# Down projection of a transformer layer as seven block products over two chunks, added to the residual out of PSUM

## What is computed

```python
def hybrid_layer(x, ...):
    ...
    x = x + mixed @ w_out
    h = rms_norm_2(x, mlp_norm_w)
    return x + jnp.square(jax.nn.relu(h @ w_up)) @ w_down
...
for layer in range(DEPTH_2):          # DEPTH_2 = 2
    x = hybrid_layer(x, ...)
return rms_norm_2(x, final_norm_w)
```

## Time and profile before

| | us |
|---|---|
| median of 3 runs | 2745.24 (2744.96 to 2747.38) |
| the profiled execution, its own time | 2742.98 |
| its span, first to last instruction | 2740.9 |
| TensorE busy in the span | 2535.8 (93%) |
| VectorE busy | 1757.3 (64%) |
| ScalarE busy | 1214.6 (44%) |
| stretch of the first layer's feed-forward part | 1676.85 to 2026.91 |
| stretch of the second layer's | 2377.20 to 2727.23 |

### The profile page before, as it was taken

The page is one execution under the profiler, slowest core; times in us unless marked ns, Lnnn a source line. Parts: engine busy times, 40 slices in busy tenths (PEclk is TensorE's granted clock), DMA queues, the critical chain, the costliest instruction groups (busy, mean ns, idle before and its releaser), DMA issues.

```text
span 2740.9 us, 32380 instructions
## 1 busy us (share of the span) xinstructions
PE 2535.8 (93%) x11843; PEld 1995.5 (73%) x11843; DVE 1757.3 (64%) x2579; ACT 1214.6 (44%) x1747; POOL 154.6 (6%) x186
## 2 busy tenths in 40 slices
PE   5899999999987999999699899999999989999998
PEld 2776877777775878787576567888887656788886
DVE  5466566786856989998648864444443886444445
ACT  5432355555333777776442463222243336423222
POOL 0111000000000111111000000000000100000000
PEclk8999999999998999999899899999999999999999
DMA  6457535454433999998334432232233443222331
GB/s 224 162 194 252 150 98 151 119 147 142 162 130 123 364 373 366 359 349 309 133 100 123 121 91 93 92 102 97 92 98 100 137 118 94 75 96 92 96 100 72
DMA packets 229560, 431.54 MB, mean 157 GB/s; under 512 B 63380, under 2 KB 86435, under 8 KB 229442
## 3 DMA queue, kind: packets, MB, share of 16 engines
q1 hardware_dynamic: 211978, 386.83, 42.7%
q0 software_dynamic: 17232, 43.02, 4.6%
q10 hardware_dynamic: 232, 0.14, 0.0%
HBM read 399.00 MB, written 46.68 MB: 163 GB/s over the span
## 4 chain that ended last, share of the span: by engine, by line
PE 63%; DVE 18%; DMA 8%; ACT 5%; issue 4%; SPq 1%; POOL 0%; DVEq 0%; ACTq 0%; POOLq 0%
PE BKP L825 29%; PE BKP L1039 5%; PE BKP L847 4%; PE BKP L845 4%; PE BKP L846 4%; DVE WL L3026 3%; DMA W<-in_w_expert_gu_dram 2%; DVE G L3140 2%; PE BKP L1169 2%; DVE TOP L3138 2%; PE BKP L1083 2%; ACT WH L1979 2%; DVE hL L3026 1%; DMA G<-in_w_expert_gu_dram 1%; PE TPP L1070 1%
## 5 line engine op out<-in xcount | busy, mean ns | idle before, releaser
L2239 DVE TENSOR_TENSOR WL<-W,WH 128x2048 fp32r<-128x2048 f32 x126 | 288.7, 2292 | 351.8 <-ACT WH L1534 349.5
L1534 ACT ACTIVATE WH<-W 128x2048 fp32r<-128x2048 f32 x126 | 241.1, 1914 | 565.2 <-PE BKP L825 284.5
L825 PE MATMUL BKP<-hH,WH 128*128 128x512 f32 x896 | 354.5, 396 | 12.0 <-ACT Z L1593 2.7
L825 PE MATMUL BKP<-hL,WH 128*128 128x512 f32 x896 | 349.4, 390 | 0.0
L825 PE MATMUL BKP<-hH,WL 128*128 128x512 f32 x896 | 348.8, 389 | 0.0
L825 PEld LDWEIGHTS BKP<-hH,WH 128*128 128x128 f32 x896 | 168.2, 188 | 59.4 <-issue 15.0
L847 PE MATMUL BKP<-WH,aL 128*128 128x512 f32 x512 | 199.2, 389 | 0.0
L845 PE MATMUL BKP<-WH,aH 128*128 128x512 f32 x512 | 199.2, 389 | 0.0
L846 PE MATMUL BKP<-WL,aH 128*128 128x512 f32 x512 | 199.2, 389 | 0.0
L825 PEld LDWEIGHTS BKP<-hL,WH 128*128 128x128 f32 x896 | 168.2, 188 | 36.0
L825 PEld LDWEIGHTS BKP<-hH,WL 128*128 128x128 f32 x896 | 168.4, 188 | 33.6
(11 more groups left out here) (573 smaller groups left out, 5534.7 us busy)
## 6 DMA issues: line engine op xcount, KB each, us to landing
W<-in_w_expert_gu_dram SPq DMA_DIRECT2D x46, 1024.0 KB, 7.5
G<-in_w_expert_gu_dram SPq DMA_DIRECT2D x46, 1024.0 KB, 7.6
W<-in_w_in_dram SPq DMA_DIRECT2D x42, 1024.0 KB, 5.2
W<-in_w_up_dram SPq DMA_DIRECT2D x32, 1024.0 KB, 5.1
W<-in_w_down_dram SPq DMA_DIRECT2D x32, 1024.0 KB, 5.1
W<-in_w_expert_down_dram SPq DMA_DIRECT2D x24, 1024.0 KB, 6.7
G<-in_w_expert_down_dram SPq DMA_DIRECT2D x22, 1024.0 KB, 6.8
X<-in_w_mod_dram SPq DMA_DIRECT2D x16, 1024.0 KB, 7.7
```

The lines of the kernel that those rows point to most:

```text
L825: mm = pe.matmul(BK[j][:, 0:cols], lt, rh, start=start and a == 0, stop=stop and a == len(q) - 1, skip_group_check=True)
L1534: act.activation(WH[s][:], W[s][:] if raw is None else raw, ACT.Copy).then_inc(sems["w_hi"], 1)
L2239: v.tensor_tensor(WL[s][:], W[s][:] if raw is None else raw, WH[s][:].bitcast(F32), ALU.subtract).then_inc(sems["w_lo"], 1)
```

## The change

Two chunks are taken together. Their down projection is a product of a 512 x 1024 matrix of hidden values and a 1024 x 1024 matrix of weights. Hidden values are cut into four blocks (chunk by half of the tokens, `HQ[chunk][half]`, 256 tokens each), weights into four (chunk by half of the output columns), and the output into four quarters of `X` (half of the tokens by half of the columns, `X11`, `X12`, `X21`, `X22`). Seven products of sums and differences of such blocks take the place of the eight direct ones. Four differences of weight blocks (`weights_made`) and four sums or differences of hidden rows (`rows_made`) are made by VectorE.

A product `q` has its own weight pair (`WH3`, `WL3`: now three places in a ring, the third on `Z` and `AT`) and its own operand pair (`OPH`, `OPL`: three places). It adds into one of three pairs of PSUM banks (`FOLD`): A is `SC`, B is `TP`, C is `BK[2]` and `BK[3]`. A chain of products goes on adding in the same bank, and after each product VectorE adds the sum as it then stands to a quarter of `X` (`to_x`). A product's two halves wait for their bank's `sc_free` or `tp_free`, which `to_x` raises.

The hidden values are now finished before they are rounded: VectorE takes max(PSUM, 0) times the token's norm factor into `HR` (`evacuated`; `RTOK` holds the factors along the columns, spread by four small matmuls and a copy), and ScalarE squares in place (`squared`). `SQUARE` becomes the root of what it was (`roots` in place of a reciprocal). Raw weight blocks go round four places (`raw_units`); differences are written over raw blocks that are no longer needed, one into `TBUF`. The loops over chunks become code written out for four pairs per layer on every engine. Between the layers the transposes of two column blocks stand ahead of the last product, two behind it (`folded_blk`). In the last layer the root and scaling of tiles 0 and 1 stand between the adds of products 5 and 6. Some semaphores are shared under new names (`op_hi`, `op_lo`, `sig_sq`, `rows_made`), and some small tensors are put side by side to get the space.

The diff, cut to its core and moved to the left (in order: names; bank pairs and raw places; SyncE; TensorE; ScalarE; VectorE):

```diff
+by4 = lambda ap: ap.rearrange("p (k n) -> p k n", k=UK)
+WH3, WL3 = [WH[0][:], WH[1][:], by4(ZR)], [WL[0][:], WL[1][:], by4(ATR)]
+HR, HQ = [ST[0], ST[1]], [[ST[c][:, :, t * 256:(t + 1) * 256] for t in range(2)] for c in range(2)]
+SA, SB3, TBUF = by4(flat(F[:])), by4(QSB[:]), by4(BIG[:, 0:UK * UN])
+OPH = [by4(flat(aH[:])[:, 0:1024]), by4(flat(aH[:])[:, 1024:2048]), by4(BIGR[:, 2048:3072])]
+OPL = [by4(flat(aL[:])[:, 0:1024]), by4(flat(aL[:])[:, 1024:2048]), by4(BIGR[:, 3072:4096])]
+RTOK = flat(VSB[:])[:, 0:S]
+GFN = flat(W[0][:])[:, 0:D]
+TBL = [TP[:, 0:512], TP[:, 512:1024], BK[2], BK[3], TP[:, 0:512], TP[:, 512:1024], SC[:, 0:512], SC[:, 512:1024]]
...
+PAIRS = ["sc_free", "tp_free"]
+NPAIR, UPAIR = FF // UN // 2, 11
+FOLD = [("A", True), ("B", True), ("A", False), ("B", False), ("A", False), ("C", True), ("A", False)]
+FOLD_BANKS = {"A": [(SC[:, 0:UN], "sc_free"), (SC[:, UN:], "sc_free")],
+              "B": [(TP[:, 0:UN], "tp_free"), (TP[:, UN:], "tp_free")],
+              "C": [(BK[2], BANKS[2]), (BK[3], BANKS[3])]}
+def raw_units(g, s):
+    ring = [(W[1 - s][:], f"w_landed{1 - s}"), (G[:, 0:4, :], "w_landed2"), (G[:, 4:8, :], "w_landed3")]
+    return (W[s][:], f"w_landed{s}"), ring[g % 3], ring[(g + 1) % 3], ring[(g + 2) % 3]
...
+def get(raw, m, src):
+    sp.wait_ge(sems["w_lo"], first + m + 2)
+    load(raw[0], src.rearrange("(k p) n -> p k n", p=P), raw[1])
+for g in range(NPAIR):
+    m = UPAIR * g
+    a, b, c, d = raw_units(g, s)
+    up = lambda ch, k: pick(t["w_up_2"], l)[k * UN:(k + 1) * UN, (2 * g + ch) * UN:(2 * g + ch + 1) * UN]
+    dn = lambda ch, hf: pick(t["w_down_2"], l)[(2 * g + ch) * UN:(2 * g + ch + 1) * UN, hf * UN:(hf + 1) * UN]
+    get(a, m - 5 if g else -2, up(0, 0))
+    get(b, m - 4 if g else -1, up(0, 1))
+    get(c, m - 2 if g else 0, up(1, 0))
+    get(d, m - 1 if g else 0, up(1, 1))
+    get(a, m, dn(0, 1))
+    get(b, m + 1, dn(0, 0))
+    get(c, m + 2, dn(1, 0))
+    get(d, m + 3, dn(1, 1))
...
+def folded(q, o, s):
+    pe.wait_ge(sems["w_lo"], T.next("w_lo"))
+    pe.wait_ge(sems["op_lo"], T.next("op_lo", 2 if q == 1 else 1))
+    banks, opens = FOLD[q]
+    for tt, (bank, free) in enumerate(FOLD_BANKS[banks]):
+        pe.wait_ge(sems[free], T.next(free))
+        cols = slice(tt * P, (tt + 1) * P)
+        for k in range(UK):
+            pe.matmul(bank, OPH[o][:, k, cols], WH3[s][:, k, :], start=opens and k == 0, stop=False,
+                      skip_group_check=True)
+            pe.matmul(bank, OPH[o][:, k, cols], WL3[s][:, k, :], start=False, stop=False, skip_group_check=True)
+            mm = pe.matmul(bank, OPL[o][:, k, cols], WH3[s][:, k, :], start=False, stop=k == UK - 1,
+                           skip_group_check=True)
+        mm.then_inc(sems["gemm_done"], 2)
...
+def folded_blk(form, n):
+    def rest(j):
+        if j == 0:
+            pe.wait_ge(sems["x4"], 3 * NT)
+            for k in range(4, NK):
+                turned_x(k, TBL[k])
+    for k in (2, 3):
+        pe.wait_ge(sems[BANKS[k]], T.at(BANKS[k]))
+        turned_x(k, TBL[k])
     unit(h, 0, form, n, True, False, ready="norm_lo", each=rest)
...
+def factors_spread(j):
+    if j == 0:
+        pe.wait_ge(sems["norm_rd"], 2 + 2 * l + 2)
+        for i in range(NT):
+            mm = pe.matmul(SC[:, i * P:(i + 1) * P], SQUARE[:, i:i + 1].to_broadcast([P, P]), IDN[:],
+                           start=True, stop=True, skip_group_check=True)
+        mm.then_inc(sems["row_pe"], 1)
+        T.skip("row_in")
+for g in range(NPAIR):
+    m = UPAIR * g
+    if g == 0:
+        normed_blk(at=(at(0), at(1)), each=factors_spread)
+    else:
+        unit(h, 0, "F", UN, True, False, at=at(m))
+        unit(h, 4, "F", UN, False, True, at=at(m + 1))
+    unit(h, 0, "F", UN, True, False, at=at(m + 2))
+    unit(h, 4, "F", UN, False, True, at=at(m + 3))
+    for q in range(7):
+        if g == NPAIR - 1 and q == 6 and l == 0:
+            pe.wait_ge(sems["norm_xn"], T.next("norm_xn", NT))
+            for k in range(2):
+                turned_x(k, TBL[k])
+        folded(q, (7 * g + q) % 3, at(m + 4 + q))
...
+def rounded(m, src):
+    act.wait_ge(sems["gemm_done"], g0 + (1 if m == 2 else 4 * (m - 2)))
+    act.activation(WH3[ring[m % 3]], src, ACT.Copy).then_inc(sems["w_hi"], 1)
+def squared(c, j):
+    act.wait_ge(sems[BANKS[j]], T.next(BANKS[j]))
+    act.activation(HR[c][:, j, :], HR[c][:, j, :], ACT.Square).then_inc(sems["sig_sq"], 1)
+def operand(g, q, src, made, ks=slice(0, UK)):
+    n = 7 * g + q
+    if n >= 3:
+        act.wait_ge(sems["gemm_done"], g0 + 4 * (UPAIR * g + (q + 2 if q >= 3 else q - 2)))
+    if made:
+        act.wait_ge(sems["rows_made"], T.next("rows_made", made))
+    act.activation(OPH[n % 3][:, ks, :], src[:, ks, :], ACT.Copy).then_inc(sems["op_hi"], 1)
...
+rounded(m + 3, d[0])
+if g == 0:
+    landed(b, c)
+    T.skip("norm_rd")
+    act.wait_ge(sems["row_pe"], T.next("row_pe"))
+    act.activation(RTOK, SC[:, 0:S], ACT.Copy).then_inc(sems["row_in"], 1)
...
+landed(d)
+act.wait_ge(sems["tw_made"], T.next("tw_made", 2))
+rounded(m + 5, a[0])
+for j in range(3):
+    squared(1, j)
+operand(g, 1, SA, 2, slice(0, 2))
+squared(1, 3)
+operand(g, 1, SA, 1, slice(2, 4))
+act.wait_ge(sems["tw_made"], T.next("tw_made"))
+rounded(m + 6, a[0])
+operand(g, 2, HQ[0][0], 1)
+rounded(m + 7, c[0])
+operand(g, 3, SA, 1)
+rounded(m + 8, TBUF)
+operand(g, 4, SB3, 0)
+rounded(m + 9, d[0])
+act.wait_ge(sems["sig_sq"], T.next("sig_sq", 4))
+operand(g, 5, HQ[1][0], 0)
+act.wait_ge(sems["tw_made"], T.next("tw_made"))
+rounded(m + 10, b[0])
+operand(g, 6, HQ[1][1], 0)
...
-link(v.reciprocal(SQUARE, SM[:, 3, 0:4]))
+roots(SQUARE, m4, half4, work4)
+v.sem_inc(sems["norm_rd"], 1)
...
+def remainder(m, src):
+    v.wait_ge(sems["w_hi"], T.next("w_hi"))
+    r = ring[m % 3]
+    v.tensor_tensor(WL3[r], src, WH3[r].bitcast(F32), ALU.subtract).then_inc(sems["w_lo"], 1)
+    T.skip("w_lo")
+def evacuated(m, c, j):
+    v.wait_ge(sems["gemm_done"], g0 + 4 * m + j + 1)
+    v.scalar_tensor_tensor(HR[c][:, j, :], BK[j], 0.0, RTOK, ALU.max, ALU.mult).then_inc(sems[BANKS[j]], 1)
+    T.skip(BANKS[j])
+def operand(n, src, ks=slice(0, UK)):
+    v.wait_ge(sems["op_hi"], T.next("op_hi"))
+    v.tensor_tensor(OPL[n % 3][:, ks, :], src[:, ks, :], OPH[n % 3][:, ks, :].bitcast(F32),
+                    ALU.subtract).then_inc(sems["op_lo"], 1)
+def rows_made(dst, a, b, op, ks=slice(0, UK)):
+    v.tensor_tensor(dst[:, ks, :], a[:, ks, :], b[:, ks, :], op).then_inc(sems["rows_made"], 1)
+def weights_made(dst, a, b):
+    v.tensor_tensor(dst, a, b, ALU.subtract).then_inc(sems["tw_made"], 1)
+    T.skip("tw_made")
+x_rows = lambda first, hf: [X[:, i, hf * UN:(hf + 1) * UN] for i in (first, first + 1)]
+X11, X12, X21, X22 = x_rows(0, 1), x_rows(0, 0), x_rows(2, 1), x_rows(2, 0)
+def to_x(g, q, dst, since, last=False):
+    for tt, (bank, free) in enumerate(FOLD_BANKS[FOLD[q][0]]):
+        v.wait_ge(sems["gemm_done"], g0 + 4 * (UPAIR * g + 4 + q) + 2 * (tt + 1))
+        if tt == 0:
+            v.wait_ge(sems[since], T.at(since, 0))
+        v.tensor_tensor(dst[tt], dst[tt], bank, ALU.add).then_inc(sems[free], 1)
+        if last:
+            v.wait_ge(sems[free], T.at(free))
+            v.sem_inc(sems["x4"], 1)
+        T.skip(free)
+a, b, c, d = raw_units(0, s)
+remainder(1, b[0])
+for g in range(NPAIR):
+    last = g == NPAIR - 1
...
+if g:
+    to_x(g - 1, 6, X21, BANKS[3])
+remainder(m + 2, c[0])
+remainder(m + 3, d[0])
+if g == 0:
+    v.wait_ge(sems["row_in"], T.next("row_in"))
+else:
+    weights_made(TBUF, c[0], b[0])
+for j in range(4):
+    evacuated(m + 1, 0, j)
+remainder(m + 4, a[0])
+operand(n, HQ[0][0])
+if g == 0:
+    weights_made(TBUF, c[0], b[0])
+weights_made(a[0], b[0], a[0])
+v.wait_ge(sems["sig_sq"], T.next("sig_sq", 4))
+rows_made(SB3, HQ[0][0], HQ[0][1], ALU.subtract)
+remainder(m + 5, a[0])
+weights_made(a[0], c[0], a[0])
+evacuated(m + 3, 1, 0)
+v.wait_ge(sems["tw_made"], T.at("tw_made", 0))
+weights_made(b[0], d[0], a[0])
+evacuated(m + 3, 1, 1)
+evacuated(m + 3, 1, 2)
+v.wait_ge(sems["sig_sq"], T.next("sig_sq", 2))
+rows_made(SA, HQ[0][1], HQ[1][1], ALU.add, slice(0, 2))
+evacuated(m + 3, 1, 3)
+operand(n + 1, SA, slice(0, 2))
+v.wait_ge(sems["sig_sq"], T.next("sig_sq", 2))
+rows_made(SA, HQ[0][1], HQ[1][1], ALU.add, slice(2, 4))
+operand(n + 1, SA, slice(2, 4))
+rows_made(HQ[0][0], SA, HQ[0][0], ALU.subtract)
+remainder(m + 6, a[0])
+operand(n + 2, HQ[0][0])
+to_x(g, 0, X11, BANKS[3])
+remainder(m + 7, c[0])
+rows_made(SA, HQ[1][0], HQ[0][0], ALU.subtract)
+operand(n + 3, SA)
+to_x(g, 1, X22, "sc_free")
+remainder(m + 8, TBUF)
+operand(n + 4, SB3)
+to_x(g, 2, X12, "tp_free")
+remainder(m + 9, d[0])
+operand(n + 5, HQ[1][0])
+to_x(g, 3, X12, "sc_free", last)
+remainder(m + 10, b[0])
+operand(n + 6, HQ[1][1])
+to_x(g, 4, X22, "tp_free", last)
+if not last:
+    a, b, c, d = raw_units(g + 1, s)
+    remainder(m + 11, a[0])
+    to_x(g, 5, X11, "sc_free")
+    remainder(m + 12, b[0])
+elif l == 0:
```

(47 more changed lines are left out.)

244 lines of the change are left out of this document (134 added, 110 removed).

## The result

The changed kernel takes 2701.78 us (2699.00 to 2704.97), the kernel before 2745.1 beside it: a ratio of 0.9844, 95% interval 0.9830 to 0.9858. Two later sets of executions of the same kernel gave 0.985 (0.9828 to 0.9873) and 0.9864 (0.9846 to 0.9883). The forecast was 2705.4 in 2700 to 2720, that is 39.8 us less.

What follows compares the result with a forecast made beforehand. TensorE was taken to bound both MLPs throughout. Terms -43.5 (matmuls) +3 (waits) +1.8 (row factors) +0 (boundary) -1.1 (end) gave -39.8 us, a profiled execution of 2703.2 and a median of 2705.4, range 2700 to 2720.

Steps and rivals of the forecast that it cites:

- TensorE alone bounds both parts, and 192 matmuls are 43.5 us: Both MLPs: TensorE is busy throughout; 24 fewer matmuls per pair, 5.44 us each, over 8 pairs save 43.5 us.
- Waits, 3 us, at q=3 alone: TensorE waits before q=3 on VectorE's add: 0.2 us per pair, 0.5 in each layer's first; sum 2.2, taken as 3.
- The walk: Step-by-step timing of VectorE and ScalarE through one later pair; it found q=3 the tightest place, 0.2 us late.
- Rival A: VectorE's overlap between operations is lost at semaphore waits: waits 10.6 us instead of 3, about 2713 us; chance 0.20.
- Rivals B: ScalarE's handoffs to VectorE are not covered: 1.23 us each, 15 per pair, 120 in all, 2822 us; chance 0.06.
- C: Uncovered handoffs in part, or late loads or fetches, eat 4 us or more per pair: 2716 to 2739; chance 0.10.
- D: Such losses eat 5.4 us per pair and nothing changes: within 5.5 us of 2745; chance 0.04.
- Row factors, 1.8: Four small matmuls and a copy per layer spread the row factors, holding TensorE 0.92 us: +1.8 us for two layers.
- Between the layers 0: Boundary between the layers: 5.85 us before, 5.9 walked after, so zero change, plus or minus 1.5 us.
- at the end -1.1: After TensorE stops, the last scaling ends 9.6 us later instead of 10.7: -1.1 us, between -2.5 and +1.
- Strided operand reads at the plain price: VectorE reads operands as rows of 256 out of 512 columns; priced like plain reads, nothing added.
- of the same form: The products' 168 matmuls per pair match the old 192 in form (128x128 stationary, 512 columns), each priced at 0.2267 us.

Runs made afterwards that it cites:

- experiment 2: Changed kernel with each pair's first product computed twice, putting back 24 matmuls per pair: MLPs +21.78 and +21.67 us, ratio 1.0007 to the kernel before.
- experiment 5: Changed kernel with MODP, CF and KS0 moved so ATR begins at 128 modulo 8192: each MLP 1.65 us less; in a later run 2700.16 us against 2703.17.
- experiment 3: Changed kernel with one more VectorE instruction per pair, a 128x1024 sum of 1.21 us ahead of the q=1 adds to X: 2711.77 us against 2701.97.
- experiment 4: Changed kernel with MODP moved ahead of F, so ATR begins at a multiple of 64 bytes: second layer's MLP 331.4 to 331.1 us, ratio 0.9836 to the kernel before.

## Why the prediction was right, step by step

**TensorE alone bounds both parts, and 192 matmuls are 43.5 us.** Right, to 0.1: experiment 2 puts them back for 43.45.

**Waits, 3 us, at q=3 alone.** The place was right, the size was not: by the starts the changed kernel waits 0.07 or less around q=3 in each pair, 0.25 in both layers. This is the term that was mis-sized, and two things lie under it. The walk took 0.75 us for an evacuation, from the nearest row with a scalar per partition; groups of the kernel after, with the columns of the earlier trace rows:

```profile
L3432 DVE SCALAR_TENSOR_TENSOR ST<-BKP,VSB 128x512 f32<-128x512 f32 x64 | 42.4, 684 | 26.3 <-PE BKP L875 19.5 <-ACT VSB L2303 6.8
L3456 DVE TENSOR_TENSOR X<-X,SCP 128x512 f32<-128x512 f32 x64 | 41.7, 680 | 4.3 <-PE SCP L911 3.5 <-DVE X L3456 0.2
```

At 0.684 the walk, which has four of them ahead of the adds of q=1, has these adds 0.2 to 0.3 earlier. In a later pair that starts at 1759.00, VectorE in fact does this (timeline):

```profile
1811.33 1.28 DVE L3456 TENSOR_TENSOR X<-X,SCP 128x512 f32<-128x512 f32 x2
1812.53 2.28 DVE L3426 TENSOR_TENSOR WL<-G,WH 128x2048 fp32r<-128x2048 f32 x1
1814.73 1.22 DVE L3442 TENSOR_TENSOR F<-ST 128x1024 f32<-128x1024 f32 x1
1817.13 1.23 DVE L3438 TENSOR_TENSOR aL<-F,aH 128x1024 fp32r<-128x1024 f32 x1 [1.19 <-ACT aH L2285]
1818.28 1.28 DVE L3456 TENSOR_TENSOR X<-X,TPP 128x512 f32<-128x512 f32 x2
```

The second product's adds start 59.28 us into the pair (59.2 in the walk, and the pair itself is 0.5 longer by then). The second thing is the slow third buffer, which hid what was left; experiment 5 uncovers 0.15 to 0.2 per pair, the walk's 0.2. Its 0.5 for first pairs was too much: they lose 0.2 there, like the others.

**Rival A, no overlap on VectorE.** It falls. In the rows above each operation that follows straight on another starts 0.07 to 0.09 before the recorded end of the one before it, also where its program waits for a semaphore in front (L3426 at 1812.53, L3456 at 1818.28). The Trainium skill, "VectorE: DVE Perf Modes", section "The DRAIN you can't avoid", says that the next operation doesn't start until the pipe is empty, and adds that one which isn't held starts earlier; the prediction gave the first half alone. These rows show the earlier start.

**Rivals B, C and D.** They fall. ScalarE's hand-offs cost nothing even with two operand buffers, and no load or fetch appears among TensorE's waits in these parts. The cover is thin in one place only, q=3 (experiment 3). C's condition and its range didn't belong together: 4 us per pair would have given about 2734, and 2716 takes only 1.7 per pair.

**Row factors, 1.8.** 1.6: timeline of TensorE after, the four small matmuls and the next matmul, 0.81 per layer.

```profile
2368.96 1.05 PE L1566 MATMUL SCP<-IDN,MODP 128*128 128x128 f32 x8
2369.77 0.48 PE L875 MATMUL BKP<-hH,WH 128*128 128x512 f32 x1
```

**Between the layers 0, at the end -1.1.** Measured -0.1 and -1.07. **Strided operand reads at the plain price.** Right: 1.22 in the rows above for L3442, which reads rows of 256 out of 512 columns.

**What the sum lacked: the place of a buffer, +4.0 us.** The text says that the products are "of the same form" and prices each at 0.2267. They are of the same form, but 18 of 56, and ten of the up units, read weights from a buffer that lies differently. That is also why pairs repeat every 82.0 to 82.3 us (first products of the first layer at 1720.71, 1802.95, 1884.97 and 1967.13) where the text says 81.6 to 82; in experiment 5's layout they repeat at 81.8. So the sum of -39.8 came near the measured -38.4 partly by luck: 2.7 us too many of waits stood against 4.0 us that it did not know.

## What to carry to other kernels

Where one engine is busy for the whole of a stretch, count its instructions first and then walk the order of the others through one turn with recorded overlaps; that walk found the one place that can wait, to 0.2 us. Prices from a near row with another operand (a scalar per partition for an immediate) are worth a correction, because four of them ahead of one add decided whether there was a wait here. When a change brings a new buffer, compare where it begins with where the buffers beside it begin, and look for a matmul spacing that changes with the buffer's name and not with the step.

## What was not expected of the hardware

The spacing of 512-column matmuls depended on where their weights begin: 0.2267 us at 128 modulo 1024 bytes for all, 0.231 where the second half of the weights begins 32 bytes off a multiple of 64 (0.229 in products where it begins at 0 modulo 1024, experiment 4), 0.2342 in products and 0.2333 in up units where both halves do. No wait and no change of the granted clock (1.00) shows in the profile; only the distances between starts tell it. And the start of one and the same stage, 1.67 ms into the program, moves by up to 9 us between profiles of kernels that share all that comes before it, while a stage bound by TensorE repeats to 0.03 us.
